# Two transformer blocks on one core: the activation buffers 320 bytes further on in SBUF, the mixers' buffer 32 bytes lower by remainder of 512

## What is computed

```python
h = rmsnorm(x, g) * (1 + scale) + shift            # per stage, from c @ w + b
ffn:   x += 0.5 * gate * ((silu(h @ w_gate) * (h @ w_up)) @ w_down)       # 1024 -> 2816 -> 1024
mamba: z, xbc, dt = split(h @ w_in); y = ssd_scan(silu(conv4(xbc)), dt)   # 32 heads of 64, state 128
       x += gate * (rmsnorm(y * silu(z)) @ w_out)
attn:  x += gate * (mix(h @ w_qkv) @ w_out)        # 16 heads of 64, mix is softmax or stick-breaking
cffn:  x += gate * ((silu(conv3(h @ w_up)[:F]) * conv3(h @ w_up)[F:]) @ w_down)
```

## Time and profile before

| | |
|---|---|
| median of 3 runs | 1866.17 us (1860.8 to 1866.32) |
| the profiled execution | 1859.02 us, span 1857.2 us |
| TensorE matmul busy | 95% of the span, 14608 instructions |
| VectorE, ScalarE busy | 78%, 52% |
| mean granted TensorE clock | 0.982 |

### The profile page before, as it was taken

One profiled execution on the slowest core, in us unless ns is written; L12 is line 12 of the kernel. 1 busy time (PEld: TensorE's weight loads), 2 busy tenths in 40 slices (PEclk: granted clock), 3 DMA queues, 4 the chain that ended last, 5 costly groups with the idle time before them and its releaser, 6 DMA issues.

```text
span 1857.2 us, 34057 instructions
## 1 busy us (share of the span) xinstructions
PE 1758.6 (95%) x14608; PEld 1703.8 (92%) x14608; DVE 1440.3 (78%) x1714; ACT 961.6 (52%) x1257; POOL 0.2 (0%) x4
## 2 busy tenths in 40 slices
PE   4999999999999999999989999898998999989999
PEld 4999999998899999999979999888898988889999
DVE  7799887787799879986557998655799777448676
ACT  4433466666443453445564434655644556666554
POOL 0000000000000000000000000000000000000000
PEclk9999999999999999999999999999999999999999
DMA  9999734433599859983426997243395535324551
GB/s 396 417 410 365 291 114 159 158 138 136 192 384 364 325 199 379 368 325 134 164 109 229 386 370 302 93 159 114 130 342 186 202 139 178 129 92 168 195 189 46
DMA packets 68149, 426.23 MB, mean 229 GB/s; under 512 B 7488, under 2 KB 10832, under 8 KB 31824
## 3 DMA queue, kind: packets, MB, share of 16 engines
q1 hardware_dynamic: 63936, 416.22, 58.4%
q10 hardware_dynamic: 4112, 8.62, 1.4%
HBM read 423.74 MB, written 3.17 MB: 230 GB/s over the span
## 4 chain that ended last, share of the span: by engine, by line
PE 84%; DVE 10%; ACT 3%; issue 2%; DMA 1%; DVEq 0%; SPq 0%; ACTq 0%
PE bank L1414 24%; PE bank L1416 24%; PE bank L1415 24%; DVE w_lo L840 3%; PE bank L1487 2%; DVE macc L881 2%; PE bank L1427 1%; PE bank L1429 1%; PE bank L1755 1%; DMA mix<-mods 1%; DVE mix L1042 1%; PE bank L1434 1%; PE bank L1597 1%; PE bank L1736 1%; DVE mix L858 1%
## 5 line engine op out<-in xcount | busy, mean ns | idle before, releaser
L1414 PE MATMUL bank<-h_hi,w_hi 128*128 128x256 f32 x2864 | 802.3, 280 | 13.7 <-DVE w_lo L840 12.9
L1415 PE MATMUL bank<-h_lo,w_hi 128*128 128x256 f32 x2864 | 796.0, 278 | 0.0
L1416 PE MATMUL bank<-h_hi,w_lo 128*128 128x256 f32 x2864 | 796.0, 278 | 0.0
L840 DVE TENSOR_TENSOR w_lo<-raw,w_hi 128x2048 fp32r<-128x2048 f32 x276 | 631.6, 2289 | 134.7 <-ACT w_hi L441 134.2
L441 ACT ACTIVATE w_hi<-raw 128x2048 fp32r<-128x2048 f32 x276 | 528.0, 1913 | 145.8 <-PE bank L1416 133.6
L1414 PEld LDWEIGHTS bank<-h_hi,w_hi 128*128 128x128 f32 x2864 | 541.9, 189 | 18.5 <-DVE w_lo L840 14.7
L1415 PEld LDWEIGHTS bank<-h_lo,w_hi 128*128 128x128 f32 x2864 | 540.7, 189 | 0.1
L1416 PEld LDWEIGHTS bank<-h_hi,w_lo 128*128 128x128 f32 x2864 | 540.8, 189 | 0.0
L1414 PE MATMUL bank<-a_hi,w_hi 128*128 128x256 f32 x1280 | 357.6, 279 | 0.0
L1416 PE MATMUL bank<-a_hi,w_lo 128*128 128x256 f32 x1280 | 354.7, 277 | 0.0
L1415 PE MATMUL bank<-a_lo,w_hi 128*128 128x256 f32 x1280 | 354.7, 277 | 0.0
(11 more groups left out here) (261 smaller groups left out, 1653.5 us busy)
## 6 DMA issues: line engine op xcount, KB each, us to landing
raw<-weights SPq DMA_DIRECT2D x276, 1024.0 KB, 5.0
modws<-mods SPq DMA_DIRECT2D x144, 768.0 KB, 6.9
mix<-mods SPq DMA_DIRECT2D x5, 1024.0 KB, 8.8
mix<-mods ACTq DMA_DIRECT2D x8, 512.0 KB, 13.8
biases<-scratch ACTq DMA_DIRECT2D x1, 2048.0 KB, 13.9
mix<-biases ACTq DMA_DIRECT2D x4, 512.0 KB, 3.9
modws<-mods SPq DMA_DIRECT2D x1, 1024.0 KB, 11.8
x<-xin SPq DMA_DIRECT2D x1, 1024.0 KB, 10.9
```

The lines of the kernel that those rows point to most:

```text
L840: eng.tensor_tensor(w_lo[g % NW][:, :], raw[g % NRAW][:, :], w_hi[g % NW][:, :], ALU.subtract).then_inc(sems["wlo"], 1)
L1414: eng.matmul(dst, ah, bh, start=start, stop=False, skip_group_check=skip)
L1415: eng.matmul(dst, ah, bl, start=False, stop=False, skip_group_check=skip)
L1416: return eng.matmul(dst, al, bh, start=False, stop=stop, skip_group_check=skip)
```

## The change

Only addresses move; no instruction is added, dropped or reordered on any engine. `cact` (320 bytes) is allocated ahead of `h_hi` instead of behind `small`. So `h_hi`, `h_lo`, `work`, `modws`, `macc`, `modv`, `par`, `con`, `conb`, `ws_hi`, `ws_lo` and `small` lie 320 bytes further on, and `rstd`, `sel` and `acg` stay. A new `gap` of 320 bytes moves `a_hi` and `a_lo` by the same. `shift` goes, and `gap2` of 704 bytes takes its place, so that `mix` lies 992 bytes further on (1024 less 32).

```diff
         gs = sb("gs", [P, NJOB, 8])
+        cact = sb("cact", [P, NJOB * 8])
         h_hi = sb("h_hi", [P, KT, T], F32R)
...
         small = sb("small", [P, 12])
-        cact = sb("cact", [P, NJOB * 8])
         rstd = sb("rstd", [P, T])
         sel = sb("sel", [64, 512], F32R)
 
         acg = sb("acg", [64, 384], F32R)[:, :]
+        gap = sb("gap", [P, 80])
         a_hi = sb("a_hi", [P, 2, T], F32R)
         a_lo = sb("a_lo", [P, 2, T], F32R)
         z_hi, z_lo = h_hi[:, 0:2, :], h_lo[:, 0:2, :]
-        shift = sb("shift", [P, 8])
+        gap2 = sb("gap2", [P, 176])
         mix = sb("mix", [P, 6144])
```

## The result

The changed kernel takes 1923.7 us (median of 4 runs, 1921.91 to 1927.19) against 1863.6 us for the kernel before (median of 4 runs, 1860.8 to 1866.32), a ratio of 1.031 with a 95% interval of 1.0273 to 1.0346. The forecast was 1849, the range ended at 1899.

The account below looks back on a forecast made before the run. TensorE, busy 95% of the span, was taken as the bound: matmul count times pitch. From the profiled 1859.0 us, 12.9 us gained less 3 us left out gave -10, the other parts 0: 1849 us, range 1841 to 1899.

Parts of the forecast that it names:

- the other engines, the DMA queues and the mixers' buffer: VectorE and ScalarE hidden behind TensorE, DMA unchanged, `mix` and `con` moves: each taken as 0, the last with 5.7 us either side.
- V blocks and ordinary ones become alike: Block matmuls: operand distances of 64, or 448 in V blocks, all become 256, so both kinds get the same pitch.
- the first of the parts: `h` and `a` from 448 to 256 in all blocks: most long pitches become short, -12.9 us, less 3 us left out.
- The reading of two streams that meet: TensorE's 117.7 ns pitch: the moving stream and the next stationary load meet in the same part of SBUF.
- the bound: Block matmuls' worst case: all short pitches become long, 9900 x 4.4 ns = +43.6 us.
- the new distance is a bad one: Rival: streams meet in every block matmul, feed-forward stages lose the short pitch; 1868 to 1903 us, chance 0.33.
- a new pitch would make its sizes wrong: Sign in the trace: a pitch neither 113.3 nor 117.7 ns keeps the reading of streams meeting but makes the sizes wrong.
- addresses have no say: Rival: block pitches do not depend on addresses, or are redrawn evenly; 1859 to 1866 us, chance 0.20 with the even case.
- a stall in the 113.3 ns: Rival: the short pitch holds a stall over 106.7 ns of columns that 256 apart removes; 52 us, 1794 us, chance 0.05.
- the eight-column products: TensorE's products with eight stationary columns: 113.3 ns at six different distances, taken as the floor of this kind of matmul.
- 2,900 matmuls run at the long pitch: Mamba stage, V blocks and parts of attention and sparse stages: 4.4 ns too long each, costing 12.9 us.
- a stage that settles otherwise: One feed-forward stage at the long pitch costs 7.0 us, matching the runs' median 7.1 us above the profiled execution.

Follow-up runs that it names:

- e3: Kernel before with only the weight slots `w_hi` and `w_lo` moved by 192 bytes, operands 256 apart, activations unmoved by remainder of 512; 1923.5 us, ratio 1.0317.
- e1: Kernel before with only the mixers' buffer moved, by taking out the 32 unused bytes of `shift`; 1860.1 us, ratio 0.9983.
- e2: Kernel before with `h` and the buffers behind it moved to 256 from the weight slots, `a` and the mixers' buffer keeping their remainders; 1906.8 us, ratio 1.0227.
- e9: Kernel before with only the `w_lo` slots moved by 192 bytes, to distance 256; `w_hi` stays at 448; 1901.0 us, ratio 1.0203.
- e12: Kernel before with three extra matmuls ahead of the Mamba stage's gate, x and z blocks, their result overwritten; 1869.0 us against 1861.5, one run each.
- e10: Kernel before with `h` and `a` moved 256 bytes, to distance 192, the mixers' buffer keeping its remainder; 1864.1 us, ratio 1.0000.

## Why the prediction was wrong

**Right:** that only TensorE's pitch could change the time; that the pitch depends on where the two operands lie to each other and not on where one of them lies (e3); that the other engines, the DMA queues and the mixers' buffer count for nothing (e1, against the page after); that V blocks and ordinary ones become alike.

**The step that failed** is the first of the parts: the new distance was priced from the norm's matmul, ones and `work` 256 apart, 216 ns for 213 ns of columns. That row does not carry over. It is full fp32, at 216 ns for 256 columns, while the fp32r matmuls have 113.3 to 120.0 ns for as many: half their rate. The fp32r matmuls themselves lose nothing to the distance at half their rate: at the lower clock they have 213.4 ns before and after. Whether full fp32 depends on the distance no run tests, since ones and `work` stay 256 apart in all of them. What the runs show in its place: fp32r at the upper clock has 120.0 ns at a distance of 256, 6.7 ns more than at 448 (e2, e3). The row that did carry over stood in the prediction and was read for another purpose: the extra matmuls, fp32r with both operands at 0. By the period of 256 that is the new distance, and its 117 ns, disturbed by the change of distance on either side, were a hint at 120. The reading of two streams that meet fits all this and e9's eight blocks, but no run shows it to be the cause.

**The second failure is the bound.** The rival "the new distance is a bad one" named the case that came true, with 0.33, and was sized by the two pitches that the trace of before has: at worst all at 117.7, +43.6 us and 1903. The real one was a third, 120.0, so that a short step grew by 6.7 ns instead of 4.4 and a long one by 2.2 instead of nothing. 9,943 x 6.7 + 2,967 x 2.2 = 73 us, of which some 10 us came back. The prediction said at its end that a new pitch would make its sizes wrong, but gave that no price above; an end of the range that is worked out from values seen at two distances is no bound for a third.

**The other rivals.** That addresses have no say fell with e3. The rule of the Trainium skill that was put beside it ("TensorE: Matmul & The Clock Gate", Part 2: two independent read ports, so that a weight load takes no bandwidth from the running matmul) does not decide the time here: the same fp32r matmuls at the same clock differ by 6.7 ns by the distance of their operands alone (e3). Whether it is the ports that the runs contradict, or something behind them, is not shown. That a stall in the 113.3 ns could be removed fell with the table, in which nothing is shorter.

**Smaller slips:** the kernel has 277 blocks, the first of them split in halves, where the prediction counts 276. The granted clock is not at its upper level in every slice: a slice hides stretches at 0.5, as 152 to 156 us. And the eight-column products are no floor: their 24 matmuls have 116.9 ns a step after the change and in e2 and e3, though their own distances by remainder of 256 are as before. The estimate that 2,900 matmuls run at the long pitch was good (2,967 steps), and so was its reading that the runs of one kernel can differ by a stage that settles otherwise: e12 shows such a stage, e12 being one trace.

## What to carry to other kernels

Where TensorE is the bound and its matmuls are like these (fp32r, 128 stationary and 256 moving columns, the clock at its upper level), the SBUF addresses of the two operands are a tuning parameter: here it was worth 6% of each matmul, 113.3 against 120.0 ns. What counted was their distance by remainder of 256 bytes. The nearest distances tried on either side of the good one, 16 bytes away, had lost it, so a tensor added ahead of one of the two can cost 3% of the kernel. Other types and shapes were not tried. Read the pitch block by block from the starts in the trace, and try several distances in one run by giving each buffer of a rotation another remainder.

A price for a condition that the trace does not have must come from the same kind of instruction at the same rate, and its range must be open beyond the values that other conditions show.

## What the runs showed of the hardware that I had not expected

- The pitch has a period of 256 bytes in the distance: 120.0 ns at 0 and at 256, 118.3 at 224 and at 480, 116.8 at 32 and at 288, 113.3 or 117.8 at 192 and at 448. Exchanging the operands' roles changed only the sign of the distance, to within 1.3 ns.
- It is not smooth: 176, 192 and 208 have 119.3, 113.3 and 119.1 ns.
- At 192 two pitches are stable, one of them for up to 1,489 matmuls in a row. An uninterrupted stretch keeps the one that it begins with, in 296 of 296 (e12). At 0 there is one alone.
- At the lower clock, 1.2 GHz, the distance makes no difference: 213.4 ns a matmul at 448 and at 256.
- Moving the mixers' buffer by 32 bytes, with nothing else changed, gave 1,169 more block steps under 116 ns (e1, one trace of each). e10, where that buffer keeps its remainder, has 308 more. Neither is enough for the time of the runs to tell.
